# Recurrent states of eight running samples, updated between the steps of the prompt's chunks

## The reference

```python
def mlstm_chunk(carry, blk):                 # carry: C (H x DK x DV), n (H x DK), m (H)
    b = jnp.cumsum(lf, axis=-1)
    dmat = where(causal, b[:, None] - b[None, :] + ig[None, :], -inf)
    s = einsum('bhtd,bhsd->bhts', q, k) * exp(dmat - m_row)
    num = w_prev * einsum('bhtd,bhde->bhte', q, C) + einsum('bhts,bhse->bhte', s, v)
    den = w_prev * einsum('bhtd,bhd->bht', q, n) + s.sum(-1)
    h = num / maximum(abs(den), exp(-m_row))
    C_new = decay * C + einsum('bhsd,bhse->bhde', wk, v)
    n_new = decay * n + wk.sum(2)
    return (C_new, n_new, m_new), h

# prompt: a scan of mlstm_chunk over chunks, one state; each needs the one before
# samples: mlstm_chunk with one token each, eight states (C, n, m) read and written back
```

## Time and profile before

| | us |
|---|---|
| median of three runs | 3512.46 |
| lowest, highest run | 3499.12, 3525.58 |
| profiled execution, its span | 3545.2 |
| stage `mlstm` in it, L737's first start to L809's first start, layer 0 | 115.5 |
| the same, layer 1 | 106.75 |
| of it from the end of the last chunk's L773 to L809, layer 0 and 1 | 43.6 and 34.3 |

### The profile page before, as it was taken

The page is one execution under the profiler, slowest core; times in us unless marked ns, Lnnn a source line. Parts: engine busy times, 40 slices in busy tenths (PEclk is TensorE's granted clock), DMA queues, the critical chain, the costliest instruction groups (busy, mean ns, idle before and its releaser), DMA issues.

```text
span 3545.2 us, 69005 instructions
## 1 busy us (share of the span) xinstructions
PE 3315.6 (94%) x27968; PEld 3061.3 (86%) x27968; DVE 1331.5 (38%) x1838; ACT 1096.7 (31%) x1595; POOL 133.7 (4%) x168
## 2 busy tenths in 40 slices
PE   8999999988888999999999999998988899899998
PEld 7999988767666998999999998986776689899997
DVE  3333344356222444333333334444642224433333
ACT  2222243144332324222232213332433323332213
POOL 0000000000221000000000000000012300000000
PEclk9999999699998999999999999998999999999998
DMA  5322231111542322322133222301034423222221
GB/s 133 90 86 80 71 79 33 33 30 49 188 168 92 89 86 66 89 87 82 57 96 89 86 80 54 96 16 50 26 101 176 175 59 95 65 81 85 86 84 55
DMA packets 443313, 296.31 MB, mean 84 GB/s; under 512 B 24328, under 2 KB 430572, under 8 KB 434986
## 3 DMA queue, kind: packets, MB, share of 16 engines
q1 hardware_dynamic: 430265, 217.05, 21.8%
q0 software_dynamic: 12928, 77.64, 5.9%
HBM read 286.44 MB, written 8.34 MB: 83 GB/s over the span
## 4 chain that ended last, share of the span: by engine, by line
PE 85%; ACT 5%; DVE 4%; another core or an unknown queue 4%; issue 2%; DMA 0%; DVEq 0%; SPq 0%; ACTq 0%
PE ps L619 64%; PE ps L966 3%; PE ps L1002 2%; PE ps L668 2%; PE ps L647 1%; PE ps L981 1%; PE ps L659 1%; PE ps L912 1%; ACT res L1200 1%; ACT x_hi L1199 1%; DVE ckv_t L1774 1%; PE ps L1016 1%; PE ps L903 1%; ACT prob L1365 1%
## 5 line engine op out<-in xcount | busy, mean ns | idle before, releaser
L1492 DVE TENSOR_TENSOR w_lo<-w_raw,w_hi 128x1024 fp32r<-128x1024 f32 x436 | 533.8, 1225 | 1082.9 <-ACT w_hi L1166 1082.9
L619 PE MATMUL ps<-x_hi,w_hi 128*128 128x268 f32 x4032 | 839.4, 289 | 34.0 <-DVE x_lo L1531 25.7
L1166 ACT ACTIVATE w_hi<-w_raw 128x1024 fp32r<-128x1024 f32 x436 | 460.7, 1057 | 1226.3 <-PE ps L619 1214.2
L619 PE MATMUL ps<-x_lo,w_hi 128*128 128x268 f32 x4032 | 829.6, 287 | 0.0
L619 PE MATMUL ps<-x_hi,w_lo 128*128 128x268 f32 x4032 | 828.2, 287 | 0.0
L619 PEld LDWEIGHTS ps<-x_hi,w_hi 128*128 128x128 f32 x4032 | 631.8, 189 | 42.6 <-DVE x_lo L1531 33.3
L619 PEld LDWEIGHTS ps<-x_lo,w_hi 128*128 128x128 f32 x4032 | 634.4, 189 | 0.0
L619 PEld LDWEIGHTS ps<-x_hi,w_lo 128*128 128x128 f32 x4032 | 631.3, 189 | 0.0
L619 PE MATMUL ps<-h_hi,w_hi 128*128 128x268 f32 x1408 | 294.6, 291 | 0.6 <-DVE w_lo L1492 0.3
L619 PE MATMUL ps<-h_hi,w_lo 128*128 128x268 f32 x1408 | 290.3, 288 | 0.0
L619 PE MATMUL ps<-h_lo,w_hi 128*128 128x268 f32 x1408 | 289.4, 287 | 0.0
(11 more groups left out here) (361 smaller groups left out, 3699.3 us busy)
## 6 DMA issues: line engine op xcount, KB each, us to landing
w_raw<-in_ffn_up SPq DMA_DIRECT2D x180, 512.0 KB, 3.8
w_raw<-in_w_in SPq DMA_DIRECT2D x72, 512.0 KB, 3.8
w_raw<-in_ffn_down SPq DMA_DIRECT2D x64, 512.0 KB, 3.7
w_raw<-in_ffn_down SPq DMA_DIRECT2D x32, 384.0 KB, 3.1
w_raw<-in_w_o SPq DMA_DIRECT2D x16, 512.0 KB, 3.7
c_smp<-in_state_C SPq DMA_DIRECT2D x16, 256.0 KB, 2.9
out_new_C_sample<-c_smp SPq DMA_DIRECT2D x16, 256.0 KB, 2.4
w_raw<-in_w_pa SPq DMA_DIRECT2D x16, 256.0 KB, 2.7
```

Of the source, the lines that this page charges most:

```text
L619: ins = mm(ps[0:m, 2 * p + half, 0:HT], w[:, s, off + t_ * m:off + t_ * m + m], x[part][:, k0 + t_, half * HT:(half + 1) * HT], start=firs ...
L1166: f(w_hi[:, s, :], w_raw[:, s, :], ACT.Copy).then_inc(hi_made, 1)
L1492: v.tensor_tensor(w_lo[:, s, :], w_raw[:, s, :], w_hi[:, s, :].bitcast(F32), ALU.subtract).then_inc(lo_made, 1)
```

## The change

The samples' part after the chunks is dissolved. Its preparation (L781, L782, the turn of `n_in`, and what ScalarE and VectorE make of it) goes ahead of the first chunk, into bank 5. Each sample's update goes into a chunk: samples 0, 1, 3, 4, 6, 7 in the middle of chunks 0 to 5 (`SMP_MID`), samples 2 and 5 at the end of chunks 1 and 3 (`SMP_END`). TensorE's spreading of v is `sample_rows(b)`, its product with q is `sample_out(b)`, one chunk later, and VectorE's three operations are `sample_state(b)`. The 12 fillers per sample are gone. The chunk's denominator moves from bank 5 to bank 0, since bank 5 now holds a sample's v; so the products that build the next decay matrix must wait until ScalarE has read the denominator (`ch_abs`), and they move behind L743 and L745. The turn of the prompt's `n` stays behind the last chunk, with a semaphore of its own (`np_turned`). SP's list of loads and stores is unchanged.

```diff
+SMP_MID, SMP_END = (0, 1, 3, 4, 6, 7), (None, 2, None, 5, None, None)
...
@@ tensor, mlstm
+                for h in range(HA):
+                    one_h = ident[0:HA, h:h + 1].to_broadcast([HA, P])
+                    mm(ps[:, 5, h * 24:h * 24 + 16], one_h, row_we[:, :, NP_TOK:TOK], start=True, stop=True)
+                    mm(ps[:, 5, h * 24 + 16:h * 24 + 24], one_h, row_a[:, NP_TOK:TOK], start=True, stop=True)
+                turn(ps[:, 5, 96:96 + DEC * HA], n_in[:, :], ident[0:DEC * HA, 0:DEC * HA]).then_inc(smp_bc_made, 1)
+
                 def chunk_in(c):
...
-                    mm(ps[0:CH, 0, 0:HA * CH], row_a[:, sl], ident[0:HA, 0:HA].unsqueeze(2).to_broadcast([HA, HA, CH]), start=True, stop=False)
-                    for h in range(HA):
-                        mm(ps[0:CH, 0, h * CH:(h + 1) * CH], ident[0:HA, h:h + 1].to_broadcast([HA, CH]), row_p[:, sl], start=False, stop=False)
-                    mm(ps[0:CH, 0, 0:HA * CH], ident_b[:, :], mask_b[:, :].unsqueeze(1).to_broadcast([CH, HA, CH]), start=False, stop=True).then_inc(ch_in, 1)
 
                     for h in range(HA):
                         mm(ps[0:CH, 1, h * CH:(h + 1) * CH], qk[:, HA + h, sl], qk[:, h, sl], start=True, stop=True)
                     for h in range(HA):
                         ins = turn(ps[0:CH, 6, h * P:(h + 1) * P], qk[:, HA + h, sl], ident[:, :])
                     ins.then_inc(ch_in, 1)
+
+                    if c:
+                        pe.wait_ge(ch_abs, l * NCH + c)
+                    mm(ps[0:CH, 0, 0:HA * CH], row_a[:, sl], ident[0:HA, 0:HA].unsqueeze(2).to_broadcast([HA, HA, CH]), start=True, stop=False)
...
                     keep_warm(2, 5)
+                    if c == 1:
+                        pe.wait_ge(n_rows_made, l * 2 + 1)
...
+                def sample_rows(b):
+
+                    if b:
+                        pe.wait_ge(c_new, l * DEC + b)
+                    else:
+                        pe.wait_ge(n_made, l + 1)
+                    row_b = ident_r[:, b:b + 1].to_broadcast([DEC, P])
+                    mm(ps[:, 5, :], row_b, v_hi[:, :, :], start=True, stop=False)
+                    mm(ps[:, 5, :], row_b, v_lo[:, :, :], start=False, stop=True).then_inc(c_vb, 1)
+
+                def sample_out(b):
+
+                    pe.wait_ge(c_new, l * DEC + b + 1)
+                    for h in range(HA):
+                        ins = mm(ps[:, 2, HA * CH + h * DEC + b:HA * CH + h * DEC + b + 1], c_smp[:, b % 4, h, :], qk[:, h, NP_TOK + b:NP_TOK + b + 1], start=True, stop=True)
+                    ins.then_inc(c_read, 1)
+
                 chunk_in(0)
-                keep_warm(5, 24)
+                keep_warm(4, 24)
                 for c in range(NCH):
 
-
+                    sample_rows(SMP_MID[c])
                     pe.wait_ge(ch_own, l * NCH + c + 1)
...
+                    if SMP_END[c] is not None:
+                        sample_rows(SMP_END[c])
+                    if c == 0:
+                        mm(ps[:, 3, HA * CH:HA * CH + HA * DEC], ones[:, :], q_n[:, :, :], start=True, stop=True, skip_group_check=True).then_inc(n_den, 1)
+                        turn(ps[0:DEC * HA, 3, 384:384 + P], n_bh[:, :, :], ident[:, :]).then_inc(n_den, 1)
+                    else:
+                        sample_out(SMP_MID[c - 1])
+                        if SMP_END[c - 1] is not None:
+                            sample_out(SMP_END[c - 1])
                     if c + 1 < NCH:
-                        keep_warm(0, 5)
+                        keep_warm(6, 5)
                         chunk_in(c + 1)
+                last = NCH - 1
+                sample_out(SMP_MID[last])
 
                 pe.wait_ge(ch_done, l * NCH + NCH)
...
+                turn(ps[0:HA, 4, 0:P], c_st[:, :, DK], ident[:, :]).then_inc(np_turned, 1)
...
-                for b in range(DEC + 1):
-                    if b < DEC:
...
-                        keep_warm(1, 12, 256)
...
@@ scalar, mlstm
+                    if c == 0:
+                        act.wait_ge(n_den, l * 2 + 2)
+                        f(s_den[:, :, :], ps[:, 3, HA * CH:HA * CH + HA * DEC].rearrange("p (h b) -> p h b", h=HA), ACT.Abs).then_inc(n_abs, 1)
+                        f(n_rows[:, :], ps[0:DEC * HA, 3, 384:384 + P], ACT.Copy).then_inc(n_rows_made, 1)
...
@@ vector, mlstm
                     v.tensor_tensor(q_wn[:, :, :], q_w[:, :, :], c_st[:, :, DK:DK + 1].to_broadcast([P, HA, CH]), ALU.mult).then_inc(ch_mix, 1)
+                    sample_state(SMP_MID[c])
                     dve.wait_ge(ch_out, l * NCH + c + 1)
...
                     v.tensor_tensor(qk[:, 0:HA, sl], ps[:, 4, 0:HA * CH].rearrange("p (h t) -> p h t", h=HA), r_den[:, :, :], ALU.mult).then_inc(ch_done, 1)
...
+                    if SMP_END[c] is not None:
+                        sample_state(SMP_END[c])
```

More of the change, by code:

```diff
@@ L764, in mlstm @@
                         pe.wait_ge(ch_done, l * NCH + c)
-                    mm(ps[:, 5, 0:HA * CH], ones[0:CH, :], s_m[:, :, :], start=True, stop=False, skip_group_check=True)
+                    mm(ps[:, 0, 0:HA * CH], ones[0:CH, :], s_m[:, :, :], start=True, stop=False, skip_group_check=True)
                     for h in range(HA):
@@ L772, in mlstm @@
                         mm(ps[:, 4, h * CH:(h + 1) * CH], c_st[:, h, 0:DK], q_w[:, h, :], start=False, stop=True, skip_group_check=True)
-                    mm(ps[:, 5, 0:HA * CH], ones[:, :], q_wn[:, :, :], start=False, stop=True, skip_group_check=True).then_inc(ch_out, 1)
+                    mm(ps[:, 0, 0:HA * CH], ones[:, :], q_wn[:, :, :], start=False, stop=True, skip_group_check=True).then_inc(ch_out, 1)
+                    if SMP_END[c] is not None:
+                        sample_rows(SMP_END[c])
@@ L1617, in mlstm, with sample_state @@
                 step.then(v.memset(c_st[:, :, :], 0.0))
+                sm = slice(NP_TOK, TOK)
+                dve.wait_ge(smp_bc_read, l * 2 + 2)
+                v.tensor_tensor(k_w[:, :, :], qk[:, HA:, sm], smp_bc[:, :, 2, :], ALU.mult)
+                step.then(v.tensor_tensor(n_st[:, :, :], n_st[:, :, :], smp_bc[:, :, 0, :], ALU.mult))
+                step.then(v.tensor_tensor(n_st[:, :, :], n_st[:, :, :], k_w[:, :, :], ALU.add))
+                v.tensor_tensor(q_n[:, :, :], qk[:, 0:HA, sm], n_st[:, :, :], ALU.mult).then_inc(n_made, 1)
+                def sample_state(b):
+                    dve.wait_ge(c_loaded[b % 4], (l * 2 + b // 4 + 1) * 16)
+                    c_ = c_smp[:, b % 4, :, :]
+                    step(v.tensor_tensor(c_, c_, smp_bc[:, :, 0, b:b + 1].to_broadcast([P, HA, DK]), ALU.mult))
+                    dve.wait_ge(c_vb, l * DEC + b + 1)
+                    step.then(v.tensor_tensor(c_add[:, :, :], ps[:, 5, :].rearrange("p (h d) -> p h d", h=HA),
+                                              k_w[:, :, b:b + 1].to_broadcast([P, HA, DK]), ALU.mult))
+                    v.tensor_tensor(c_, c_, c_add[:, :, :], ALU.add).then_inc(c_new, 1)
+                    dve.wait_ge(c_new, l * DEC + b + 1)
                 for c in range(NCH):
@@ L1639, in mlstm @@
                     v.tensor_tensor(qk[:, 0:HA, sl], ps[:, 4, 0:HA * CH].rearrange("p (h t) -> p h t", h=HA), r_den[:, :, :], ALU.mult).then_inc(ch_done, 1)
-                sm = slice(NP_TOK, TOK)
-                dve.wait_ge(smp_bc_read, l * 2 + 2)
-                v.tensor_tensor(k_w[:, :, :], qk[:, HA:, sm], smp_bc[:, :, 2, :], ALU.mult)
-                step.then(v.tensor_tensor(n_st[:, :, :], n_st[:, :, :], smp_bc[:, :, 0, :], ALU.mult))
-                step.then(v.tensor_tensor(n_st[:, :, :], n_st[:, :, :], k_w[:, :, :], ALU.add))
-                v.tensor_tensor(q_n[:, :, :], qk[:, 0:HA, sm], n_st[:, :, :], ALU.mult).then_inc(n_made, 1)
-                for b in range(DEC):
-                    dve.wait_ge(c_loaded[b % 4], (l * 2 + b // 4 + 1) * 16)
-                    c_ = c_smp[:, b % 4, :, :]
-                    step(v.tensor_tensor(c_, c_, smp_bc[:, :, 0, b:b + 1].to_broadcast([P, HA, DK]), ALU.mult))
-                    dve.wait_ge(c_vb, l * DEC + b + 1)
-                    step.then(v.tensor_tensor(c_add[:, :, :], ps[:, 5 + b % 2, :].rearrange("p (h d) -> p h d", h=HA),
-                                              k_w[:, :, b:b + 1].to_broadcast([P, HA, DK]), ALU.mult))
-                    v.tensor_tensor(c_, c_, c_add[:, :, :], ALU.add).then_inc(c_new, 1)
-                    dve.wait_ge(c_new, l * DEC + b + 1)
+                    if SMP_END[c] is not None:
+                        sample_state(SMP_END[c])
                 dve.wait_ge(n_abs, l + 1)
```

39 lines of the change are left out of this document (12 added, 27 removed).

## The result

The changed kernel takes 3530.7 us (median of 20 runs, 3519.05 to 3540.38) against 3505.98 us for the kernel before on the same occasions (20 runs, 3479.21 to 3537.71). The ratio is 1.0065, with a 95% interval of 1.0046 to 1.0084: some 16 to 29 us slower, well inside 1%. The forecast was +24 us and "within 1%".

What follows compares the result with a forecast made beforehand. TensorE was taken to bound the kernel (85% of the chain). Stage changes of +4.9 and +13.7 us plus 5 behind it gave +23.6, put on the median 3512.46: 3536 us, 8-in-10 range 3465 to 3572.

Steps and rivals of the forecast that it cites:

- What goes: Samples' part after the last `ch_out`: 43.6 and 34.3 us per layer shrink to 3.9 each, 70.1 us gone.
- What comes in, at its price: Sample work added to the chunks: `sample_rows` 1.14 or 0.66 us, `sample_out` 1.50 or 0.79, at half or full clock.
- Covers: VectorE's 2.2 us `sample_state` fits its 2.51 us wait; new semaphore waits and transfers cost nothing.
- The clock: Assumed that more few-row work makes TensorE's clock fall in nearly every chunk; stage 120.4 us per layer.
- The start to the first `ch_out`: From the stage's start to the first chunk's `ch_out`: 22.2 us in both layers.
- the mixed second step: Second chunk step, beginning at full clock and ending at half: 13.5 us, taken between 10.6 and 19.6.
- The short returns: Brief spells of full clock during the chunks: 5.5 us per layer given back.
- After the stage: L809 and L816 begin at half clock instead of full: some 2.5 us lost per layer, 5 in all.
- The base: The difference on the 3545.2 us profiled execution was put on the median 3512.46, 33 us below it.
- Rival 1: Clock stays full through the chunks, since the new stage has even fewer gaps: 3454 us; chance 0.12.
- Rival 2: Clock behaves in the chunks as before, half for 37% and 26% of the time: 3476 us; chance 0.15.
- Rival 3: No short return at all and the clock falls before the first `ch_out`: 3568 us; chance 0.13.

Runs made afterwards that it cites:

- y1: The changed kernel with its few-row products spread among more fillers (694 products in the stage for 534); ratio 0.9952 to the kernel before.
- z1: y3 with fillers where TensorE idled: 14 ahead of the stage, 22 awaiting the last chunk, 8 awaiting `n_made`; 3478.12 us, ratio 0.9913.
- y3: The kernel before with 5 fillers added between L750 and L765, and 3 instead of 5 after a chunk; ratio 0.9935.
- x1: The changed kernel with the decay products back ahead of the k-q products and the turn of k; 3500.26 us, ratio 0.9967 to the kernel before.
- x4: The kernel before with only the decay products moved behind the k-q products and the turn of k; ratio 1.0061.
- y4: The kernel before with the 96 fillers per layer of the samples' part reading 4 of 128 rows; 3539.07 us, ratio 1.0096.
- x2: x1 with 10 fillers ahead of each `sample_rows` and 8 for 5 after a chunk; ratio 0.9932, stages 130.5 and 99.8 us.
- y2: y1 with fewer fillers: 3, 3, 2, 5, 5 and 2 for 5, 5, 4, 6, 6 and 3; ratio 1.0127 to the kernel before.
- x3: The changed kernel without the 10 fillers of each chunk, the 24 ahead of the first chunk kept; 3512.36 us, ratio 1.0008 to the kernel before.

## Why the prediction was right, step by step

- **What goes**: 43.6 us in layer 0 became 722.99 - 719.31 = 3.7 us; 3.9 was taken. Right.
- **What comes in, at its price**: a step at half clock with two samples' spreadings and one product was forecast as 17.62 + 2 x 1.14 + 1.50 = 21.4 us and measured 21.4 (636.07 to 657.51; 676.17 to 697.61); one with one spreading and two products 17.62 + 1.14 + 3.0 = 21.8, measured 21.7 (697.61 to 719.31). Right to 0.1 us, since every price was a row of the same instruction at the same clock.
- **Covers**: `sample_state` ended 2.7 us or more before L1668 could start; TensorE waited neither for `c_new` nor `ch_abs` nor `ch_own`. Right. Transfers stayed off the path.
- **The clock**: the step that carried the sign. The prediction calls it an assumption, drawn from what TensorE had done ahead of three falls. The start to the first `ch_out` took 22.4 us (22.2 forecast), the mixed second step 14.4 (13.5). The short returns were mis-sized: I gave back 5.5 us per layer, there was one return of 3.4 us in each layer, and the step that held it in layer 0 was 18.7 instead of 21.8 long, so 3.1 us. The 5.5 was a guess between two bounds; no row gave it. Together the stage was 3.3 us longer than my 120.4. The mean clock, 0.56, was at the low end of "0.55 to 0.6".
- **After the stage**: from the head norm's first product to the next stage's it took 741.06 - 722.99 = 18.1 us in layer 0, and 729.47 - 714.19 = 15.3 before: +2.8, and +1.4 in layer 1; 5 in all was forecast, 4.2 came.
- **The base**: +25.0 for the stages and +4.2 behind them is 29 us in the profiles; the medians differ by 24.7. I had put the difference on the median although the profiled execution lay 33 us above it. That was luck: what made it long lay in the paged attention and not in the stage, and nothing that I had looked at said so. It is luck too that 23.6 forecast and 24.7 measured lie so close: on the profile, for which the sum was worked out, 23.6 stands against 29, and the runs of the kernel before spread over 58 us, so one profile of it need not give the stage lengths of its median run.
- **Rival 1** (clock full, 3454 us) did not come. With other code the full clock is possible: y1 has 84 us of it in this very stage. Its reason, that TensorE has no gaps, is refuted by the changed kernel itself: 0.4 us idle in 123.7, clock 0.56. The Trainium skill's rule in "TensorE: Matmul & The Clock Gate", section "Why this matters for your kernels", to leave no idle gaps, agrees with one place of these traces: with 14 fillers in the gap ahead of the stage z1 began it at full clock, where y3 was at half for its first 6.8 and 13.7 us. It is not sufficient, as the changed kernel shows. By z1's other two filled gaps the samples' part gained nothing. **Rival 2** (half-clock share as before) asked for 37 and 26% between first and last `ch_out`; it was 91%: 97.6 us less 4.9 at full clock after 621.69 and 3.4 of the return. **Rival 3** (136.5 us per stage with no return and a fall ahead of the first `ch_out`) went too far: 123.7 us measured, with one return and a clock still full for the first 4.9 us of the second step. Its returns were near, 3.1 us given back where it has none and the forecast 5.5.

What is shown: with the same products, the order moves the clock and the time (x1, x4); with the same count and columns, fillers over 4 rows do not bring the clock back where those over 128 do (y4); and with enough fillers among the few-row products the clock stays full (y1, y3). What stays open: how much cover is enough, and what the products over 8 rows and those of one column do by themselves, which no run separates. Two of my estimates of the cover (x2, y2) were wrong.

## What to carry to other kernels

Work moved into the gaps of another stage is free only at the clock that the stage keeps. Before moving products that contract over few rows, lay out the order around them, and check the granted clock in the windows of the stage, not TensorE's busy share: it was 99.7% here at a mean clock of 0.56. Fillers pay where they hold the clock: enough of them held 2.4 GHz through the chunks (y1, y3), 63 fewer per layer than in y1 made the slowest kernel of all (y2), and where they do not hold the clock, taking them out is the better change (x3). The cheapest ones stand where the engine waits anyway (y3).

## What the runs showed of the hardware that was not expected

The order of the same products was worth 14 us per layer in a stage of 124 (x1 against the changed kernel). The runs of the kernel before spread over 58 us (3479 to 3538), those of the changed kernel over 21 (3519 to 3540) and of y1 over 17. A small spread does not mean that the clock is held: x4, whose clock changed twelve times in the stage of layer 1, has 13. What holds the full clock need not bring it back: in the first chunk of y1 the few-row products had the same fillers among them as later on, and the clock stayed at half until 620.40, inside the 30 fillers in a row that begin at 616.24. And the paged part of attention took 215.7 and 215.8 us in one execution and 187 to 208 in the twelve others that were profiled, with code that no edit touched; what makes it so was not tried.
